# Gate and normed slots ahead of layer 1's scan, and other orders of ScalarE, VectorE and GpSimd in both scans

## The reference

```python
px = (h_x * (1.0 + ca_x) + sa_x) @ w_in[l]
pc = (h_c * (1.0 + ca_c) + sa_c) @ w_in[l]
# A: windowed attention, q and k rotated; B: global, q and k normed, then rotated
o_b = _global_attn_latent(_rope2d(nq(qb), cos, sin), _rope2d(nk(kb), cos, sin), ...)
# C: a gated scan over the tokens, forwards and backwards, context first
f = lbd + (1.0 - lbd) * jax.nn.sigmoid(zf)        # k = 1 - f, log f the decay
s_new = jnp.exp(b_last)[..., None] * s + einsum(kc * jnp.exp(b_last[:, None] - b), vc)
o = qc * exp(b) @ s + (masked qc kc exp(b_t - b_s)) @ vc
# D: 2-D neighbourhood attention, no rotation
```

## Time and profile before

| | us |
|---|---|
| median of 3 runs | 2169.44 |
| lowest and highest | 2162.51 to 2169.88 |
| the profiled execution's own time | 2167.95 |
| its span | 2166.2 |

### The profile page before, as it was taken

One profiled execution on the slowest core, in us unless ns is written; L12 is line 12 of the kernel. 1 busy time (PEld: TensorE's weight loads), 2 busy tenths in 40 slices (PEclk: granted clock), 3 DMA queues, 4 the chain that ended last, 5 costly groups with the idle time before them and its releaser, 6 DMA issues.

```text
span 2166.2 us, 32973 instructions
## 1 busy us (share of the span) xinstructions
PE 1972.1 (91%) x12812; PEld 1680.9 (78%) x12812; DVE 1386.2 (64%) x2711; ACT 824.7 (38%) x1584; POOL 1003.2 (46%) x750
## 2 busy tenths in 40 slices
PE   6897889989998899999989989787899988999997
PEld 4796788867787788888878878687776767888786
DVE  3238789776586998999844362887966672222444
ACT  2223455356543222222243342443435633333442
POOL 1243777420154464333353335675624257655643
PEclk7999788899998899999999999998899999999999
DMA  7442010020111333333311121101120112222321
GB/s 322 152 180 98 1 40 21 21 112 2 40 59 40 118 116 117 117 119 124 128 59 69 52 98 57 52 26 40 40 112 2 40 59 78 98 97 97 117 88 68
DMA packets 26938, 177.31 MB, mean 82 GB/s; under 512 B 2720, under 2 KB 3744, under 8 KB 7712
## 3 DMA queue, kind: packets, MB, share of 16 engines
q1 hardware_dynamic: 22544, 157.90, 20.2%
q10 hardware_dynamic: 4240, 17.30, 2.0%
HBM read 171.00 MB, written 4.19 MB: 81 GB/s over the span
## 4 chain that ended last, share of the span: by engine, by line
PE 67%; DVE 19%; POOL 5%; issue 5%; ACT 3%; DMA 2%; DVEq 0%; SPq 0%; ACTq 0%; POOLq 0%
PE PS L1173 20%; PE PS L1098 17%; PE PS L851 7%; PE PS L845 5%; DVE W L1536 4%; PE PS L1034 3%; PE PS L1059 3%; PE PS L1018 2%; PE PS L948 2%; DVE W L1823 2%; DVE W L1754 2%; PE PS L1154 1%; DMA WR<-in_weights 1%; PE PS L1024 1%; PE PS L772 1%
## 5 line engine op out<-in xcount | busy, mean ns | idle before, releaser
L1173 PE MATMUL PS<-XH,WS 128*128 128x512 f32 x2016 | 548.0, 359 | 12.4 <-POOL WS L2160 10.8
L1173 PEld LDWEIGHTS PS<-XH,WS 128*128 128x128 f32 x2016 | 362.7, 191 | 69.4 <-POOL WS L2160 7.6
L1173 PE MATMUL PS<-XL,WS 128*128 128x512 f32 x1008 | 360.5, 358 | 0.0
L2160 POOL TENSOR_TENSOR WS<-WR,WS 128x1024 fp32r<-128x1024 f32 x88 | 213.9, 2433 | 314.5 <-ACT WS L1391 314.3
L1460 ACT ACTIVATE W<-PS,PR 128x768 f32<-128x768 f32 (+1 forms) x88 | 77.9, 885 | 445.3 <-PE PS L1173 383.1
L2015 DVE SCALAR_TENSOR_TENSOR W<-PS,PR,W 128x511 f32<-128x511 f32 (+1 forms) x132 | 83.0, 656 | 208.5 <-ACT W L1460 208.5
L1173 PEld LDWEIGHTS PS<-XL,WS 128*128 128x128 f32 x1008 | 192.9, 191 | 27.3
L851 PE MATMUL PS<-EU,XH 128*128 128x256 f32 x624 | 191.4, 307 | 14.3 <-issue 6.3
L1536 DVE SCALAR_TENSOR_TENSOR W<-WR,SC,W 128x256 f32<-128x256 f32 x336 | 197.1, 628 | 6.0
L2119 POOL TENSOR_TENSOR WL<-WR,EU 128x512 fp32r<-128x512 f32 x96 | 127.2, 1351 | 141.0 <-ACT EU L1233 141.0
L851 PE MATMUL PS<-WL,XH 128*128 128x256 f32 x624 | 185.3, 297 | 0.0
(11 more groups left out here) (218 smaller groups left out, 4474.9 us busy)
## 6 DMA issues: line engine op xcount, KB each, us to landing
WR<-in_weights SPq DMA_DIRECT2D x134, 1024.0 KB, 4.8
U<-in_weights SPq DMA_DIRECT2D x10, 1024.0 KB, 6.9
U<-in_bias ACTq DMA_DIRECT2D x2, 1792.0 KB, 10.1
H<-in_x SPq DMA_DIRECT2D x1, 2048.0 KB, 10.9
H<-in_x ACTq DMA_DIRECT2D x1, 2048.0 KB, 15.0
U<-in_ln_rows ACTq DMA_DIRECT2D x2, 1024.0 KB, 4.6
WR<-in_weights SPq DMA_DIRECT2D x4, 512.0 KB, 3.6
kept<-H ACTq DMA_DIRECT2D x4, 512.0 KB, 2.6
```

Of the source, the lines that this page charges most:

```text
L1173: mm = pe.matmul(PS[u.pos][:, lo:hi], w[:, part, k, :], src[:, k, lo:hi], start=(k == 0 and src is xh3 and part == 0), stop=(k == KT - 1 a ...
L2160: pool.tensor_tensor(ws5[:, u.c % 2, 1], half_slot(u), ws5[:, u.c % 2, 0], ALU.subtract).then_inc(w_low, 1)
```

## The change

Six edits:

1. `ORDERS` is the same for both layers: in layer 1 too, QB, KVB and all of FCF are own jobs ahead of the scan. QA, KVA, VD, QD and KD stay beside it.
2. In both layers FCB's four jobs run in the steps -2, -2, -1 and -1 of the loop, ahead of unit 0; in layer 0 they were own jobs. QA's first piece moves to step 0, and QA's weights are made at step -1. The pieces of layer 1 are laid out by the rule that layer 0 had.
3. PE turns the job three before, not two.
4. ACT copies the results of step i-1 ahead of the exponentials of unit i+2, not behind them.
5. DVE: `square_heads` holds the squares and sums of a normed job; `rotate` keeps the rest and is run one job later among own jobs, and one step later in the scan.
6. GpSimd looks for roots one step later. The wait ahead of QD's high weights is for one rotation fewer. The places of raw rows are counted from the layer's last rotation (`raw_of`).

```diff
-          (QC, GC, IC, FCF, FCB, QA, KVA, QB, KVB, VD, QD, KD))
+          (QC, GC, IC, QB, KVB, FCF, FCB, QA, KVA, VD, QD, KD))
...
     else:
-        mixed += forget + whole(FCB)
-        early, flow = [], [p for s in order[gate + 2:] for p in whole(s)]
+        mixed += forget
+        early, flow = whole(FCB), [p for s in order[gate + 2:] for p in whole(s)]
...
-        jobs.append((key, part, [i - 2] * PIECES))
+        jobs.append((key, part, [2 * i // len(early) - 2] * PIECES))
...
-        jobs.append((key, part, [int(t / total * UNITS) + 1 for t in steps] if gate != 3
-                     else [int(t / total * (UNITS + 1)) for t in steps]))
+        jobs.append((key, part, [int(t / total * (UNITS + 1)) for t in steps]))
...
-                j.turns = [real[n - 2]] if n >= 2 and real[n - 2].rope else []
+                j.turns = [real[n - 3]] if n >= 3 and real[n - 3].rope else []
...
+        def raw_of(j):
+            return raw[:, (j.r + 2 - (rope_end(j.l) - 1)) % 3, :]
...
-                    if ORDERS[l][at] in (QD, KD):
+                    if ORDERS[l][at] == QD:
+                        act.wait_ge(roped, rope_end(l) - 1)
+                    if ORDERS[l][at] == KD:
                         act.wait_ge(roped, rope_end(l))
-                    if ORDERS[l][at] == KD:
                         act.wait_ge(rot_tp, rope_end(l))
...
+                    take_projections(l, beside.get((l, i - 1), []))
                     if 0 <= i + 2 < len(us):
...
-                    take_projections(l, beside.get((l, i - 1), []))
                     for at, q in splits[l][1].get(i, []):
...
+            def square_heads(j):
+
+                if j.slot not in (QB, KVB):
+                    return
+                heads = 4 if j.slot == QB else 2
+                dve.wait_ge(job_act, j.after[0])
+                if j.r >= 1:
+                    dve.wait_ge(roped, j.r)
...
+                ins.then_inc(ss_ready, 1)
...
-                    if j.rope:
-                        rotate(j)
+                    if pending:
+                        rotate(pending.pop())
+                    if j.rope:
+                        square_heads(j)
+                        pending.append(j)
...
+                    for j in waiting:
+                        rotate(j)
+                    waiting = []
                     for j in beside.get((l, i - 1), []):
                         if j.rope:
-                            rotate(j)
+                            if waiting:
+                                rotate(waiting.pop())
+                            square_heads(j)
+                            waiting.append(j)
                         if j.is_e:
                             forget(j)
...
-                    head_roots(beside.get((l, i - 1), []))
+                    head_roots(beside.get((l, i - 2), []))
```

40 lines of the change are left out of this document (23 added, 17 removed).

## The result

The changed kernel takes 2147.1 us (median of 4 runs, 2145.5 to 2151.7) against 2167.3 for the kernel before it. The ratio is 0.9916, with a 95% interval of 0.9901 to 0.9931: 18 to 20 us faster. The profile is of an execution of 2145.5 us, its span 2143.7. The forecast of 2143.5 fits. Its account of where the time comes from fits only in part, as the experiments show: one edit that it gave no term is worth 24 us alone, and the one that it gave the largest term costs 12.7 us on top of the others.

What follows compares the result with a forecast made beforehand. PE was taken as the bound, busy 1972 of 2166 us, so only its idle and low-clock time could go. Layer 0's -10 and layer 1's -16 made -26 on 2167.95: 2142, as a median 2143.5, range 2124 to 2165.

Steps and rivals of the forecast that it cites:

- Prologue of layer 0: FCB beside layer 0's prologue chain: first maps 26 us after FCF's end (T0) in place of 32, 6 us gained.
- the loop's own slack takes the rest: Layer 0's loop: of 8.7 us of forget steps PE waits about 2 at unit 2; DVE's idle time absorbs the remainder.
- rival A: DVE gives back layer 0's gain, 8.7 us of forget steps paid whole; layer 1 keeps -13: 2158 us, chance 0.15.
- The port: Layer 0's loop: GpSimd's split of QA's weights slows DVE through shared SBUF access, between 0 and 4.1 us, 2 counted.
- The turn: Layer 0: later turns and rotations remove PE's 4.6 us wait for a turned block's copy; 2 us counted as gain.
- rival C: Both scans: ACT's copies ahead make exponentials wait for PE beyond 1.1 to 2 us of slack: 2190 us, chance 0.06.
- rival B: PE's 32.1 us of waits for ACT's copies go whole, full clock, layer 0 at its bound: 2129 us, chance 0.12.
- Part 2: Layer 1's new order, QB, KVB and all FCF ahead of the scan: -16 us, bounds -23 and -5.
- Own jobs: Layer 1 ahead of its scan: QB, KVB and two wide FCF jobs add 40.4 us on PE plus 1.5, 41.9.
- First maps at T0 + 41: Layer 1's prologue and context units: the first score maps, unit 4, come 41 us after FCF's end (T0).
- The rest: Layer 1 from first maps to attention: 15 spacings of 8.3 us, four context units of 5, then 13.1 us.
- p = 7.8: Layer 1's scan: lower bound of the spacing of units with outputs, near DVE's own work per unit (7.6); gives -23.

Runs made afterwards that it cites:

- fcb_own: The changed kernel with FCB's four jobs back among the own jobs of both layers, ahead of the prologue: 2149.0 us.
- copies_only: The kernel before with one edit alone, ACT copying results and turned blocks ahead of the exponentials: 2141.5 us.
- old_rotate_at_once: The changed kernel with layer 1's old slots, each rotation again right behind its squares, roots in the same step and the turn a job earlier: 2140.6 us.
- slots_only: The kernel before with only layer 1's slots in the new order, engines in their old orders: 2166.7 us.
- forgets_later: The changed kernel with FCB's two latent forget steps moved from loop steps 0 and 1 to 9 and 11, in both layers: 2153.3 us.
- copies_behind: The changed kernel with ACT's copies of results behind the exponentials again: 2153.4 us.
- l1_old_slots: The changed kernel with layer 1's slots in their old order, all engine orders as changed: 2134.4 us.

## Why the prediction was right, and where it was not

**Prologue of layer 0: right as a schedule.** Forecast: a PE gap of 6.7 us and first maps at T0 + 26. Measured, with T0 = 188.8: 6.25 us and T0 + 24.9.

```profile
200.73 0.80 PE L847 MATMUL PS<-XH,EU 128*128 128x512 f32 x1 [6.25 <-ACT U L1278]
```

**But its 8.7 us were hardly worth 8.7.** fcb_own was expected to lose 7 us in layer 0. It differs by 1.9 in the total and by 3 at layer 0's attention. The forecast named the debt, the forget steps behind unit 0's copies, and sized PE's wait at 2 us. It was 5.98:

```profile
232.21 1.12 PE L950 MATMUL PS<-W 64*128 64x64 f32 x8 [5.98 <-DVE W L1794]
```

The step in doubt is "the loop's own slack takes the rest". Of the 35 us that DVE idled in the old loop 27.6 are left in copies_only (busy for 184.2 of 211.8) and 16.6 after the change (195.7 of 212.3): the slack took most of the forget steps, and up to 4 us were paid, as the loops of fcb_own and the changed kernel differ. That is at most half of rival A, which pays 8.7 and which I gave 0.15. Another pair says less: from copies_only to old_rotate_at_once, which also puts FCB beside layer 0's prologue, layer 0's attention comes 6.9 us earlier in the profiles (425.1 against 432.0), but the medians differ by only 0.9. So the runs leave this term between 1 and 7 us.

Layer 0 as a whole gained 11.9 us where 10 were forecast. Up to 6 of them are ACT's order, for which the sum has no term: copies_only gains that much by layer 0's attention.

**The port: right in kind.** 2 us of 4.1 were counted; DVE was held for 4.4, at a place where it would have waited.

**The turn: 2 us counted for layer 0, where old_rotate_at_once lost 2.0** by its attention (425.1 against 423.1), within the spread of profiles. Most of its 6.1 us lie in layer 1, with old slots. For layer 0 alone it was not tried.

**ACT's copies: the term that was missing.** The sum has no line for edit 4; it stands in the forecast as rival C, in which it loses, with "1.1 to 2 us of slack", and within rival B. Alone it brings 24 us. I had reckoned when PE's last piece would hold up the exponentials, and not what held them up already: the row of 76.8 us, 5 us at each unit, on which the prediction has nothing. With the copies ahead ACT still waited for DVE for 66.7 us in 15 units, over 4 us in each, where rival C had 1.1 to 2 us of slack. So rival C falls away, and the 32.1 us of the earlier trace rows become time that a moved line can go for. 19.1 us of them came back in layer 1 with the old slots, and nothing with the new ones.

**Layer 1's slots: right in the scan, wrong in the sum.** -16 was forecast for Part 2 and layer 1 gained 10.6, so it looks near. But the slots alone bring nothing on the old engine orders (slots_only) and lose 12.7 us on the new ones. By steps:

- Own jobs, 41.9 forecast, 49.9 measured. The text has the condition, "while a job of 5.9 us covers one rotation with its roots": FCF's two narrow jobs of 3.1 us do not. One KVB rotation came every 5.58 us, and PE waited behind two of them and, briefly, a third. After the first two gaps a wide job took 7.1 us instead of 5.5.

```profile
1359.85 0.44 PE L931 MATMUL PS<-CN,U 128*128 128x128 f32 x2 [2.06 <-DVE U L1711]
1365.43 0.69 PE L931 MATMUL PS<-CN,U 128*128 128x128 f32 x2 [2.26 <-DVE U L1711]
```

The chain had started late: scaling by roots took 2.84 us twice, beside a weight split, where it takes 0.76 alone.

```profile
1346.10 2.84 DVE L1674 TENSOR_TENSOR U<-U,ST 128x256 f32<-128x256 f32 x2 [2.19 <-POOL ST L2083]
1348.98 2.84 DVE L1682 TENSOR_TENSOR U<-U,PR 128x256 f32<-128x256 f32 x2
...
1345.94 5.59 POOL L2147 TENSOR_TENSOR WL<-WR,EU 128x512 fp32r<-128x512 f32 x4
```

- First maps at T0 + 41 forecast, T0 + 50.6 measured. The 8.6 us of forget steps were priced for layer 0 and forgotten for layer 1, whose first four units give PE little to do. They hold up DVE's next scan (the row names L1744, the last forget step; the scan behind it ends at 1413.42), this holds up GpSimd's inputs, and behind these stand KVA's low weights, for which PE waits. With two of the steps out of the way, forgets_later had its first maps 4.6 us earlier.

```profile
1413.57 0.52 POOL L2111 TENSOR_SCALAR W<-U 128x128 f32<-128x128 f32 x1 [8.07 <-DVE U L1744]
...
1424.78 2.58 POOL L2147 TENSOR_TENSOR WL<-WR,EU 128x512 fp32r<-128x512 f32 x2
...
1427.45 0.56 PE L853 MATMUL PS<-EU,XH 128*128 128x256 f32 x1 [7.91 <-issue]
```

- The rest, 15 x 8.3 + 20 + 13.1 = 157.6 forecast, 144.7 measured. The spacing was 8.1 us in the first direction and 7.6 in the second, the context units between took 4 each, the end 10.5.

The three misses are +8.0, +9.6 and -12.9 us. The last one is not the edit of ACT: copies_behind, without it, has 144.7 us too. The shorter spacing comes with the slots, as the forecast says: slots_only has 7.7 us in the second direction with all the old orders, and l1_old_slots 9.7 and 9.8 with all the new ones. The forecast put it at 8.3, and it came near its bound of 7.8.

So the steps that failed are the price of the work ahead of the scan, put 17.6 us too low, and the missing term for ACT's order. The number was right because the first met a scan 12.9 us shorter than forecast and a gain in layer 0 that had no term: luck in the sum, though the schedule of the prologue and the direction of the spacing were right. How the gain divides depends on the path. By the copies: copies_only is -24, old_rotate_at_once adds the FCB edit of layer 0 and is not told apart from it (2140.6), the rotation adds -6, and the slots give +12.7. By the slots: slots_only is 0, the orders of the other engines with FCB beside the prologue bring it to 2153.4 (copies_behind), and ACT's order adds -6.3.

**A misread row.** The prediction divides 1453.7 - 1388.2 by seven units and gets 9.4 us for the first direction. The maps at 1453.7 are those of the seventh unit of eight, six spacings on; the eighth start at 1461.4, so the spacing was 10.5 us in both directions. This did not enter the sum. But the same miscount stands in the bound: the stretch of 60.7 us of DVE's work holds six units, not eight, and from 1388.2 to 1461.4 DVE was busy for 66.2/7 = 9.5 us per unit, not 7.6. So p = 7.8 had no support there; that DVE's work per unit fell to 54.9/7 = 7.8 us after the change is luck. And a spacing of 10.5 with PE busy for 8.8 and DVE for 9.5 per unit says that neither filled it, which was the place to read the waits of ACT. Two small slips change nothing: 5 x 5.9 + 2 x 5.5 is 40.5, and rival A's terms give 2159.

What stays open: why the two halves of the slot table give back more together behind the first maps than one by one, what FCB beside the prologue is worth in layer 0, and the 6 us of forgets_later outside the scans. The best version found is the changed kernel with layer 1's old slots, 2134.4 us.

## What to carry to other kernels

In front of each instruction of an in-order queue, look at how long that engine waits there on average; what is ready and stands behind it can go ahead of it at little cost, as long as it is shorter than that wait. When PE waits for a copy, read the waits of the engine that copies before moving PE's work. Two edits can take away the same waits, and then these are gained only once: each edit is to be priced on top of the others, not against the old trace.

## What the runs showed of the hardware

DVE's five differences, with both inputs in SBUF, were held for the time that GpSimd read SBUF and not while it only wrote: 7.48 us beside keys and split, 3.11 beside keys and a memset, 1.10 alone. The Trainium skill, SBUF — State Buffer, section "Who interferes with whom", says just this of reads and of writes alone, and the traces agree. A forget step's first instruction, one input in SBUF and 512 columns wide, took longer too, which I had not expected of it: 2.62 us beside GpSimd's keys, 0.42 at its next use.

```profile
218.46 2.62 DVE L1742 TENSOR_SCALAR U<-U 128x512 f32<-128x512 f32 x1
...
224.96 0.42 DVE L1742 TENSOR_SCALAR U<-U 128x512 f32<-128x512 f32 x1
```

TensorE's granted clock was 0.81 over the 7 us behind the two waits for rotations, so part of them at 1.2 GHz, and 1.00 (2.4 GHz) ahead of the waits and in the job after. Behind the two gaps, 4.3 us together, the wide job took 7.1 us, 1.6 more than the next.

```profile
1349.00:1354.00 5.00, 5.00 (x43) 4.84 (x41) 4.93 (x10) 0.27 (x1) 2.53 (x2) 1.00 0.00 0
...
1366.00:1373.00 7.00, 6.86 (x25) 5.21 (x24) 6.85 (x10) 0.48 (x2) 6.16 (x6) 0.81 0.00 0
1373.00:1379.70 6.70, 5.96 (x28) 4.98 (x29) 6.59 (x7) 0.89 (x2) 4.57 (x9) 1.00 0.01 2
```
